# Shift and scale rows spread by TensorE, tile 0 normed first, and two mixes moved behind tile 0's expert choice, in a two-layer trunk on one core

## The reference

```python
mod = jax.nn.silu(c) @ P['ada_w'][li] + P['ada_b'][li]
sh1, sc1, gt1, sh2, sc2, gt2 = jnp.split(mod[:, None, :], 6, axis=-1)
hm = _rmsnorm(x, P['norm1_g'][li]) * (1.0 + sc1) + sh1
...
prev = jnp.concatenate([shift0[:, None, :], h[:, :-1]], axis=1)
xx = prev - h
mix = h[None] + xx[None] * mu[:, None, None, :]
r, k, v = jnp.einsum('cbtd,cde->cbte', mix[:3], w_rkv)
xw, xa, xg = mix[3], mix[4], mix[5]
...
x = x + gt1 * out
hc = _rmsnorm(x, P['norm2_g'][li]) * (1.0 + sc2) + sh2
x = x + gt2 * _peer(hc, ...)
```

## Time and profile before

| what | value |
|---|---|
| median of 3 runs | 2942.13 us (2941.88 to 2962.33) |
| profiled execution, its own time | 2945.39 us |
| its span | 2943.5 us |
| busy: PE, DVE, POOL, ACT | 65%, 54%, 45%, 10% of the span |
| chain that ended last, shares | PE 30%, DVE 24%, DMA 21%, POOL 12%, issue 7% |
| granted TensorE clock, mean | 0.809 of full |
| DMA | 286 GB/s on average |

### The profile page before, as it was taken

How to read it: one execution, slowest core, us unless ns; L and a number is a source line. 1 busy time by engine, 2 the same in 40 slices (tenths; PEclk the granted TensorE clock), 3 DMA queues, 4 the chain that set the end, 5 groups by cost and what they waited for, 6 DMA issues and landing times.

```text
span 2943.5 us, 26768 instructions
## 1 busy us (share of the span) xinstructions
PE 1921.0 (65%) x10173; PEld 1231.3 (42%) x10173; DVE 1594.7 (54%) x2987; ACT 280.3 (10%) x442; POOL 1323.4 (45%) x1160
## 2 busy tenths in 40 slices
PE   5879857837968776657577758678257764453533
PEld 2469523327945435445245227363135433350100
DVE  4253376566752826967412146865961738766033
ACT  1111000020110010010100110001100000000000
POOL 0000012543543555655334235556754675467774
PEclk8989979968789987767798888889568986776876
DMA  8430586964679897767999878789878998899998
GB/s 275 172 130 2 189 308 202 362 238 137 202 266 348 302 325 254 242 217 235 331 355 347 315 253 322 273 281 399 294 275 340 406 386 310 279 353 371 409 409 325
DMA packets 303482, 841.78 MB, mean 286 GB/s; under 512 B 46062, under 2 KB 57246, under 8 KB 303356
## 3 DMA queue, kind: packets, MB, share of 16 engines
q0 software_dynamic: 165888, 604.05, 56.1%
q1 hardware_dynamic: 126900, 231.65, 22.3%
q10 hardware_dynamic: 10568, 4.38, 0.6%
HBM read 829.68 MB, written 10.31 MB: 285 GB/s over the span
## 4 chain that ended last, share of the span: by engine, by line
PE 30%; DVE 24%; DMA 21%; POOL 12%; issue 7%; ACT 3%; PEld 1%; SPq 0%; ACTq 0%; DVEq 0%; PEldq 0%; POOLq 0%
PE psum L1920 28%; POOL arena L721 9%; DVE arena L1125 9%; DVE arena L1105 6%; DMA arena<-in_peer_v,idx_v 6%; POOL wring L721 3%; DMA wring<-in_ada_w 3%; DMA wring<-in_gla_w_in 3%; DMA wring<-in_rw_w_rkv 2%; DMA hc<-in_peer_v,idx_v 2%; DMA wring<-in_peer_wq 1%; PE psum L1938 1%; DVE hT L1105 1%; DMA out<-arena 1%; DMA wring<-in_peer_v,idx_u 1%
## 5 line engine op out<-in xcount | busy, mean ns | idle before, releaser
L721 POOL DMA_INDIRECT arena<-in_peer_u,idx_u x560 | 740.9, 1323 | 1062.1 <-DVE acts L1125 492.7
L1920 PE MATMUL psum<-arena 128*32 128x512 f32 (+6 forms) x3662 | 610.2, 557 | 447.8 <-DMA arena<-in_peer_v,idx_v 170.5
L1125 DVE CUSTOM_DVE_ANT_0 arena<-arena,hc 128x1024 f32<-128x1024 f32 x544 | 644.1, 1224 | 90.6 <-DMA arena<-in_peer_u,idx_u 64.5
L721 POOL DMA_INDIRECT arena<-in_peer_v,idx_v x428 | 422.1, 986 | 461.4 <-PE psum L1920 340.7
L1920 PEld LDWEIGHTS psum<-arena 128*32 128x32 f32 (+2 forms) x3662 | 323.5, 170 | 665.4 <-issue 477.8
L1920 PE MATMUL psum<-pick,ident 128*128 128x256 f32 x1090 | 272.7, 405 | 47.2 <-DVEq L1376 39.2
L1920 PEld LDWEIGHTS psum<-pick,ident 128*128 128x128 f32 x1090 | 215.3, 203 | 132.6 <-issue 54.0
L1920 PE MATMUL psum<-wring,arena 128*32 128x512 f32 (+3 forms) x728 | 213.9, 663 | 77.8 <-DMA wring<-in_peer_v,idx_v 43.0
L1920 PE MATMUL psum<-hT,wring 128*128 128x128 f32 (+3 forms) x1824 | 237.9, 293 | 17.0 <-ACT arena L767 6.3
L1920 PEld LDWEIGHTS psum<-hT,wring 128*128 128x128 f32 (+1 forms) x1824 | 225.7, 198 | 40.0 <-issue 21.9
L1920 PE MATMUL psum<-wring,hT 128*128 128x512 f32 (+1 forms) x480 | 192.2, 560 | 13.5 <-DMA wring<-in_gla_w_in 10.2
(11 more groups left out here) (231 smaller groups left out, 1789.1 us busy)
## 6 DMA issues: line engine op xcount, KB each, us to landing
wring<-in_ada_w SPq DMA_DIRECT2D x24, 2048.0 KB
wring<-in_peer_wq SPq DMA_DIRECT2D x24, 2048.0 KB
wring<-in_rw_w_rkv SPq DMA_DIRECT2D x12, 2048.0 KB
wring<-in_gla_w_in SPq DMA_DIRECT2D x12, 2048.0 KB
wring<-in_rw_wo SPq DMA_DIRECT2D x6, 2048.0 KB
wring<-in_gla_wo SPq DMA_DIRECT2D x6, 2048.0 KB
vring<-mod_d SPq DMA_DIRECT2D x22, 512.0 KB
arena<-in_peer_u,idx_u POOLq DMA_INDIRECT x560, 6.2
```

The costliest lines, as they stand in the source:

```text
L721: pool.indirect_dma_start(slot(s, n), None, v_rows if side else u_rows, bass.IndirectOffsetOnAxis(index, 0)).then_inc(rows_landed[s], 16)
L1125: dve.tensor_tensor_reduce(slot(s, n), slot(s, n), hidden(li, t), 1.0, 0.0, MUL, ADD, acts[:, (3 * li + t) % 2, col:col + 1]).then_inc(row ...
L1920: return nc.tensor.matmul(out, lhsT, rhs, start=start, stop=stop)
```

## The change

At the start, SP no longer loads the prompt's shift and scale rows; TensorE multiplies the row of ones with each row into PSUM as soon as it is made. VectorE norms tile 0 and tile 1 from there and signals each tile by itself. The sample's norm, with its loaded rows, moves into `mix((0,))` between the second and the third mix. TensorE's turns and ScalarE's copies follow the same order, and 30 fillers become 4. In tile 0's choice, the release of the region (`region_free`) moves ahead of the fifth early modulation, and so do the inputs and the first two mixes of `mix((1, SAMPLE))`. SP loads the small matrices between the fifth modulation's weights and its bias rows.

```diff
--- before.py
+++ after.py
@@ -558,13 +558,10 @@
             sp.wait_ge(region_free, w.next(region_free))
             lora_inputs()
             lora_pack(lora2_first, g2_first, pack_loaded)
-            rkv(1, (0,))
+            rkv(1)
             mods_known(2)
-            for s in (False, True):
-                mod_vec(0, 1, s)
-                mod_vec(0, 0, s)
-                if not s:
-                    rkv(1, (1,))
+            mod_vec(0, 1, True)
+            mod_vec(0, 0, True)
             sp.wait_ge(norm_done, w.next(norm_done))
             sp.dma_start(sh_p[0], hc[P - 1:P, 1, :]).then_inc(shift_stored, 16)
             sp.dma_start(sh_s[0], hc[DEC_T - 1:DEC_B * DEC_T:DEC_T, SAMPLE, :]).then_inc(shift_stored, 16)
@@ -615,10 +612,12 @@
                         mod_vec(1, k)
                 queries(0)
                 if t == 0:
-                    for li, k in CHOOSE_MODS:
+                    for li, k in CHOOSE_MODS[0:4]:
                         mod(li, k)
+                    ada(*CHOOSE_MODS[4])
                     sp.wait_ge(region_free, w.next(region_free))
                     lora_inputs()
+                    mod_rows(*CHOOSE_MODS[4])
                     for i in (1, 0, 2):
                         rkv(i)
                 elif t == 1:
@@ -821,7 +820,9 @@
             def mix(tiles):
 
                 lo, n = tiles[0] * P, len(tiles) * P
-                for i in MIXES:
+                for at_, i in enumerate(MIXES):
+                    if at_ == 2 and tiles == (0,):
+                        to_hT(SAMPLE)
                     if i == 3:
                         copy_out(loraT[0:64, 0, lo:lo + n], n, 64, ACT.Tanh)
                     elif i == 4:
@@ -1062,9 +1063,9 @@
             copy_parts(0, 1)
             for k in range(2):
                 store_mod(0, k)
-            for t in range(NT):
-                to_hT(t)
+            to_hT(0)
             act.sem_inc(scalar_result, 1)
+            to_hT(1)
             mix((0,))
             core(0)
             out(0, (0,))
@@ -1315,7 +1316,7 @@
                 dve.sem_inc(vec_used, 1)
                 tt(x[:, t, :], x[:, t, :], tmp, ADD)
 
-            def mix(tiles):
+            def mix_inputs(tiles):
 
                 n = len(tiles)
                 h0 = hT[:, tiles[0]]
@@ -1333,7 +1334,15 @@
                     sT = shiftT[:, :].rearrange("p (k b) -> p k b", k=KD)
                     for c in range(COPIES):
                         tt(xs4[:, :, c * DEC_B:(c + 1) * DEC_B, 0], sT, hs4[:, :, c * DEC_B:(c + 1) * DEC_B, 0], SUB)
-                for at_, i in enumerate(MIXES):
+
+            def mix(tiles, first, last):
+
+                n = len(tiles)
+                for at_ in range(first, last):
+                    i = MIXES[at_]
+                    if at_ == 2 and tiles == (0,):
+                        adaln((SAMPLE,), True)
+                        dve.sem_inc(norm_done, 1)
                     if at_ >= 2:
                         if at_ >= 4:
                             serve()
@@ -1744,7 +1753,10 @@
                     if t < SAMPLE:
                         choose(li, t, half * PH // 2, PH // 2, CHOOSE_MODS[2 * half:2 * half + 2] if first else ())
                 if first:
+                    dve.sem_inc(region_free, 1)
+                    mix_inputs((1, SAMPLE))
                     modulations_stored(CHOOSE_MODS[3:4])
+                    mix((1, SAMPLE), 0, 2)
                     early_modulation(*CHOOSE_MODS[4])
                 if t < SAMPLE:
                     dve.wait_ge(experts_fanned, w.next(experts_fanned, 2))
@@ -1763,22 +1775,29 @@
                         build(1, 1, 1)
                 if li and t == 1:
                     add_experts(1, 0, add_tmp)
-                dve.sem_inc(region_free, 1)
+                if not first:
+                    dve.sem_inc(region_free, 1)
 
             modulation(0, 0)
             dve.wait_ge(x_loaded, w.next(x_loaded, 6 * 16))
             inverse_rms((0, 1, SAMPLE))
             modulation(0, 1)
+            shift, scale = fill(), fill()
+            for t in range(2):
+                stt(hc[:, t, :], x[:, t, :], rstd[:, 0, t:t + 1], scale, MUL, MUL)
+                tt(hc[:, t, :], hc[:, t, :], shift, ADD)
+                dve.sem_inc(operand_written, 1)
+            dve.sem_inc(vector_drained, 2)
+            steps[vector_drained.name] += 2
             modulations_stored(((0, 0), (0, 1)))
-            adaln((0, 1, SAMPLE), True)
-            dve.sem_inc(norm_done, 1)
             dve.wait_ge(scalar_result, w.next(scalar_result))
-            mix((0,))
+            mix_inputs((0,))
+            mix((0,), 0, len(MIXES))
             dve.wait_ge(scalar_result, w.next(scalar_result))
             core(0)
             out(0, (0,))
             open_rows(0, 0, 0, 64, RATES["mix"])
-            mix((1, SAMPLE))
+            mix((1, SAMPLE), 2, len(MIXES))
             rest_rows(24)
             dve.wait_ge(scalar_result, w.next(scalar_result))
             core(1)
@@ -1999,6 +2018,8 @@
                 nlora[0] += 48
                 pe.wait_ge(lora_loaded, nlora[0])
                 for at_, i in enumerate(MIXES):
+                    if at_ == 2 and tiles == (0,):
+                        h_turned((SAMPLE,))
                     pe.wait_ge(operand_written, w.next(operand_written))
                     mx = mixb[at_ % 2]
                     if i < 3:
@@ -2467,8 +2488,15 @@
             mod_sum(for_vector(), parts_of(b)).then_inc(psum_for_vector, 1)
             release(b, psum_for_vector, nfv[0])
             modulation()
-            raise_clock(30)
-            h_turned((0, 1, SAMPLE))
+            for k in range(2):
+                pe.wait_ge(mod_ready, k + 1)
+                ps = for_vector()
+                for j in range(2):
+                    last = mm(ps[:, j * 512:(j + 1) * 512], le[0:1, :], vring[0:1, bias_slot[0, k], j * 512:(j + 1) * 512])
+                last.then_inc(psum_for_vector, 1)
+            raise_clock(4)
+            h_turned((0,))
+            h_turned((1,))
             mix((0,))
             core(0)
             out(0, (0,))
```

## The result

The changed kernel took a median of 2931.91 us (2921.93 to 2941.48, 9 runs); the kernel before, in the runs of the same comparison, 2954.09 us (2941.88 to 2962.33, 9 runs). The ratio is 0.9933, 95% interval [0.9907, 0.9959]: faster by 0.7%, less than the 1% that this measurement tells from no change by itself. The profiled execution took 2938.69 us, its span 2936.6 at a mean granted clock of 0.802 (before: 2945.39, 2943.5 and 0.809).

What follows compares the result with a forecast made beforehand. No single engine was taken to bound the kernel; the chain hops between TensorE, VectorE and transfers. Gains of 16.5 at the start and 6.3 at tile 0's choice sum to 22.8: 2942.1 − 22.8 = 2919.3 us, range 2913 to 2929.

Steps and rivals of the forecast that it cites:

- the level: Whole kernel: median taken 3.3 below the profiled time, at 2942.1, so 2919.3 us after the gain of 22.8.
- Part one: Start: spread rows and the sample's norm inside the mixes bring the first wide product from 82.94 to 66.4, 16.5 gained.
- The first term: Start: TensorE's two matmuls for the scale row take 1.8 at the full clock; the other end was 3.6.
- The second term: Start: the first wide product gets no extra cost; an earlier one behind small products ran at full speed, 7.13.
- the PSUM operands: Norms of tiles 0 and 1: reading PSUM adds nothing by the rows; the skill page would give about 0.26 us.
- Part two: End of tile 0's choice: inputs and two mixes ahead of the last modulation bring the second block's product 6.3 earlier.
- the third term: End of tile 0's choice: 14 fillers queued behind the last modulation's wait take 6.31, to 475.3.
- a plain shift from there: After the first wide product: TensorE still waits 7.81 for the next weight half, so the start's gain carries on unchanged.
- Bursts start cold: Short TensorE bursts start at 1.2 GHz: scale row 1.8 more, 14 fillers up to 6.3 more; 2927.4 us, chance 0.10.
- The early loads collide: End of choice: small weights and next big half delay the last modulation, 8.2 late; 2927.5 us, chance 0.09.
- The clock never comes back: Tile 0's six wide products stay at half clock, 7.13 more each, 42.8 in all; 2962 us, chance 0.03.
- More than the sum: Rows land early, runs start warm, a later gather wait falls kindly: 27 or more gained, 2913 us, chance 0.10.

Runs made afterwards that it cites:

- all three edits: Changed kernel with its 14 fillers ahead of the last modulation's wait, two behind the sample's transposes, none ahead of tile 0's: 2929.71 us, ratio 0.9923.
- the warm product alone: Changed kernel with two filler matmuls added behind the sample tile's transposes, ahead of the first wide product: 2931.57 us, ratio 0.9923 to the kernel before.
- the spreading alone: Kernel before with TensorE spreading both prompt rows, but the sample's norm still ahead of all transposes and the choice unchanged: 2953.74 us, ratio 0.9985.
- the order alone: Kernel before with the sample's norm moved inside the mixes, prompt rows still loaded from memory with 30 fillers: 2944.25 us, ratio 0.9968.

## Why the prediction was wrong

**The step that failed is the level**: "the median lies 3.3 below the profiled time, and so 2942.1 − 22.8". The three runs shown were 2941.88, 2942.13 and 2962.33; their spread of 20 us, as large as the forecast gain, stood in the table, and I took their middle one as the kernel's time without a term for it in the range. They are the first three of the nine executions in the comparison above; the other six reach from 2944.80 to 2961.53. In the four comparisons the kernel before had medians of 2954.09, 2954.15, 2958.00 and 2953.47, 11 to 16 above. With 2954.1 in its place the same sum gives 2931.3, and 2931.91 was measured. That it comes so close is partly luck: the ratios 0.9933 and 0.9945 stand for 20 and 16 us, and the size of the gain was over-estimated too, by the rows in four terms.

**Part one, 16.5 forecast.** A shrank by 14.6, the product then cost 1.70 more: 12.9, inside the ends of 12.5 to 17.2 but near the lower. The first term is the scale row, whose two matmuls took 3.41 where I chose 1.8. My reason, that TensorE is busy ahead of them, didn't carry: it was, at a granted 1.00, and the clock fell inside the scale row all the same. In all nine profiles with the spreading it did so, and the row took 2.59 to 3.41. In the four with the 30 fillers in that place the clock was still at 1.00 when the last filler ended. Whether the single row of weights makes the difference, or the pauses of 0.30 and 0.46 that came with the two rows, no run tells. The norms were as forecast (47.22 to 52.43, 5.2), so the differences began 9.37 after the scale row's end instead of 7.75.

The four fillers, for which the sum has no term, held tile 0's transposes from 49.75 to 50.59; the differences then waited 0.50 behind tile 1's addition, which the sum had allowed for. Without them, in the kernel with all three edits, A was 23.30 against 23.52 with the warm product alone. The second term is the first wide product, at nothing in the sum and 1.70 in the run. I had argued from the earlier trace rows that small products are followed by a warm one, but there 0.77 us lay ahead of it and here 1.99. The sample's rows were no hindrance; their norm found them there at 61.01, as taken. They were the old bound, though, as the spreading alone shows.

On the PSUM operands the rows keep their verdict: the scaling took 1.28 from PSUM and 1.28 from SBUF (61.01), the addition 1.22 and 1.23. The extra that the Trainium skill (VectorE: DVE Perf Modes, "The TRN2 errata") gives a PSUM source is not seen in these float32 operations.

**Part two, 6.3 forecast.** B shrank by 4.4 (35.68 to 31.26; alone 4.4 too). The chain was the one described: modulation taken behind the mixes, then 14 fillers on the path. The fillers, the third term, were mis-sized: 7.98 instead of 6.31, at 0.51 for their first 3.5 us, behind a pause of 3.25 (I worked out 2.6). Behind 1.47, in five profiles, they took 6.31; behind 2.66 to 3.34, in four, 7.98 to 8.00. Moved ahead of the wait they took 6.31 and B fell by a further 5.4.

**The stretch between** is the fourth: the prediction carries the gain of part one to the choice as "a plain shift from there". Behind the last wide product come three short bursts on TensorE, first of the kernel before,

```profile
131.92 3.67 PE L1920 MATMUL psum<-arena 65*128 65x512 f32 x8 [1.80 <-ACT arena L767]
136.76 1.98 PE L1920 MATMUL psum<-arena,cum_mid 128*128 128x512 f32 x4 [1.17 <-ACT arena L767]
138.59 1.84 PE L1920 MATMUL psum<-half_ind,arena 128*128 128x2 f32 x16
```

and then of the changed one:

```profile
118.94 6.94 PE L1939 MATMUL psum<-arena 65*128 65x512 f32 x8 [1.79 <-ACT arena L766]
127.06 3.78 PE L1939 MATMUL psum<-arena,cum_mid 128*128 128x512 f32 x4 [1.17 <-ACT arena L766]
130.63 3.41 PE L1939 MATMUL psum<-half_ind,arena 128*128 128x2 f32 x16
```

They took 6.6 us longer, and the stretch 5.1. With 14.6 − 1.7 − 5.1 + 4.4 the second block's product is 12.2 nearer to the scale row in these two profiles. But this term is not the change's alone: in the second profile of the kernel before the three bursts took 14.1, as in the changed kernel, and the stretch 367.6.

Two slips in the prediction's figures change nothing: 27 us off 2942.1 are 2915 and not 2913, and the steps from 475.3 to 483.5 hold 0.1 to 0.3 us of gaps that it doesn't name.

**The rivals.** *Bursts start cold* happened in part, in three places of A and B: scale row +1.6, first wide product +1.70, fillers +1.67, about 5.0 in all against the 8.1 of that rival; 22.8 − 5.0 is 17.8, and the intervals give 12.9 + 4.4 = 17.3. The prediction said that no row showed the loss for so short a pause; the changed kernel's rows now do, for 1.99 us ahead of the product and 3.25 ahead of the fillers, and without the pause the same work ran at 1.00 in two experiments. The clock stood at 1.00 in the pause and fell at the start of the burst or inside it. The Trainium skill (TensorE: Matmul & The Clock Gate, "HAM oscillation") describes short runs of matmuls that are slowed because TensorE waits between them. The trace agrees for the product and the fillers, not for the scale row, ahead of which TensorE waited 0.46. *The early loads collide* did not: the modulation's halves were used 6.96 apart, 6.34 before, and the sum was ready 1.9 us before VectorE came for it. *The clock never comes back* did not: from the second product on, 7.10 to 7.13 each. *More than the sum* did not.

**Open.** What makes a burst lose the clock is not settled. The first wide product ran at full rate behind pauses of 0.30 to 1.79 (eight profiles) and lost 1.70 behind 1.90 to 2.11 (five), once each from the same code. But the short burst at 118.94 stood behind 1.79 or 1.80 in all thirteen, and took anything from 3.67 to 6.94. The stretch between the first product's end and the end of the choice follows those bursts: 364.1 to 364.7 in the four profiles in which the three took 7.5, 365.4 to 369.2 in the other nine, where they took 10.3 to 14.1. Under the new order and spreading it took 364.5 to 364.7 when the first product ran warm (three) and 366.0 to 369.2 when not (five); the kernel before, with a warm first product, took 364.1 and 367.6, so the product isn't all of it. Which bursts make the 23 us by which the tails differ isn't known either. Nor is it shown by times that the fillers ahead of the wait beat the changed kernel: 0.9917 and 0.9903 against 0.9933 and 0.9945, with intervals that overlap; by the rows they take 5.4 us out of B, and leaving the fillers out takes 6.1.

## What to carry to other kernels

A gain of some 20 us can't be added to the median of three runs that themselves spread over 20: forecast the ratio, and put the base's own scatter into the range. Where two waits stand behind each other, price each with the other one left in place: the spreading alone was worth 1 us, the order alone 7, both 14.6. When work is moved forward past a wait, look at what TensorE has just ahead of each burst that lands on the path; two fillers in a pause of 2 us gave 1.7 back, while 14 fillers behind a wait took 8 on the path to spare 1.7, and by the rows were better ahead of it or left out.

## What the runs showed of the hardware

In two profiles of one kernel TensorE was busy 1921.0 and 1960.0 us for the same 10173 instructions, at mean granted clocks of 0.809 and 0.789, and the spans differed by 21.2 us; 42 executions in one comparison reached from 2941.06 to 2975.88, over 1%. That the number of bursts at 1.2 GHz makes this scatter fits the two profiles; it is not shown for the 42. Spreading a row over 128 partitions by matmuls with a single row of weights took 1.95 us for the shift row's four instructions of 512 columns, 0.49 each, where the sixteen of a wide product with 128 rows took 7.13, 0.45 each, in the kernel with the warm first product: one row of weights was no cheaper here than 128. Both were at a granted 1.00. The granted clock fell inside the second group of such single-row matmuls in all nine profiles that have them, though TensorE had paused only 0.46 ahead of it, and the group then took 2.59 to 3.41.
